# Two-layer diffusion backbone on one core: six modulation blocks in the odd layer, softmax divisor in the turn, bias loads on ScalarE's queue

## The reference, cut to what matters

```python
def ada_modulation(cond, w_mod, b_mod):            # w_mod: 1024 x 6144, per layer
    m = jax.nn.silu(cond) @ w_mod + b_mod
    return jnp.split(m, N_MOD, axis=-1)            # sh1, sc1, g1, sh2, sc2, g2

def even_layer(...):
    h = modulate(rms_norm(x, norm_mix), sh1, sc1) @ w_in        # also for the context
    o_lat = concat([fourier_mix(u), neighbourhood_attention(q, k, v, kc, vc, rpb)])
    x = x + g1 * (o_lat @ w_out)
    x = x + g2 * swiglu(modulate(rms_norm(x, norm_ffn), sh2, sc2), w1, w3, w2)

def odd_layer(...):
    h = modulate(rms_norm(x, norm_mix), sh1, sc1) @ w_in        # q, k, v and u
    x = x + g1 * (concat([attention(q, k_all, v_all), s5_mixer(u, uc)]) @ w_out)
    x = x + g2 * moe_swiglu(modulate(rms_norm(x, norm_ffn), sh2, sc2), ...)

def one_block(q_blk):                              # both layers' softmax, in substance
    s = einsum(q_blk, k_all) * dh ** -0.5          # even layer: plus a bias cut from rpb, and a mask
    p = softmax(s)
    return einsum(p, v_all)
```

## Time and profile before

| | us |
|---|---|
| median of 3 runs | 1913.64 (1910.66 to 1914.75) |
| the profiled execution | 1914.57 |
| its span | 1912.7 |
| PE busy in it | 1814.9 (95%) |
| DVE, ACT, POOL busy | 1265.6, 1003.7, 312.3 |
| start to the end of the even layer's input projection | 0 to 163.98 |
| turn of q and k, Fourier part | 163.98 to 184.47 |
| even layer's attention | 184.47 to 262.25 |
| its output projection and dense part | 262.25 to 696.27 |
| odd layer's norm, input projection, turn | 696.27 to 789.20 |
| odd layer's attention and S5 | 789.20 to 847.70 |
| output projection, router, set-up of the experts | 847.70 to 911.13 |
| experts | 911.13 to 1912.70 |

### The profile page before, as it was taken

One profiled execution on the slowest core, in us unless ns is written; L12 is line 12 of the kernel. 1 busy time (PEld: TensorE's weight loads), 2 busy tenths in 40 slices (PEclk: granted clock), 3 DMA queues, 4 the chain that ended last, 5 costly groups with the idle time before them and its releaser, 6 DMA issues.

```text
span 1912.7 us, 25247 instructions
## 1 busy us (share of the span) xinstructions
PE 1814.9 (95%) x8938; PEld 1413.6 (74%) x8938; DVE 1265.6 (66%) x1329; ACT 1003.7 (52%) x1096; POOL 312.3 (16%) x584
## 2 busy tenths in 40 slices
PE   4999788999999989797999999999999999999998
PEld 2666444888888876465888888888888888888886
DVE  3243734442433234744998989989889898898997
ACT  3222423421312121363677767777777777776774
POOL 6887931011111124101000000000000000000000
PEclk8999899999999999897999999999999999999999
DMA  9788532122323151502799999999989999898994
GB/s 371 307 337 272 195 127 88 43 111 77 121 77 121 45 203 56 165 2 88 289 370 355 352 370 337 368 352 355 371 344 359 349 358 368 346 362 345 364 367 182
DMA packets 72374, 481.55 MB, mean 252 GB/s; under 512 B 8368, under 2 KB 11568, under 8 KB 17456
## 3 DMA queue, kind: packets, MB, share of 16 engines
q1 hardware_dynamic: 68720, 470.82, 64.5%
q0 software_dynamic: 2448, 7.61, 1.5%
q10 hardware_dynamic: 1136, 2.21, 0.4%
HBM read 473.29 MB, written 7.32 MB: 251 GB/s over the span
## 4 chain that ended last, share of the span: by engine, by line
PE 90%; DMA 3%; DVE 3%; POOL 2%; issue 1%; ACT 1%; SPq 0%; DVEq 0%; ACTq 0%; POOLq 0%
PE bank L1042 32%; PE bank L1056 16%; PE bank L775 12%; PE bank L745 4%; PE bank L804 3%; PE bank L792 3%; PE bank L625 3%; PE bank L840 2%; DMA ring<-in_ev_mod 2%; PE bank L563 2%; PE bank L1015 2%; PE bank L1025 1%; PE bank L713 1%; PE bank L605 1%; PE bank L696 1%
## 5 line engine op out<-in xcount | busy, mean ns | idle before, releaser
L1806 DVE TENSOR_TENSOR rest<-ring,WR 128x2048 fp32r<-128x2048 f32 x336 | 758.3, 2288 | 80.6 <-ACT WR L1373 80.1
L1373 ACT ACTIVATE WR<-ring 128x2048 fp32r<-128x2048 f32 x336 | 632.3, 1917 | 48.4 <-DMA ring<-in_experts 47.9
L1042 PE MATMUL bank<-WR,xer 128*128 128x512 f32 x1792 | 582.0, 397 | 0.8 <-DVE s5v L1967 0.8
L1042 PEld LDWEIGHTS bank<-WR,xer 128*128 128x128 f32 x1792 | 337.0, 188 | 70.3 <-issue 0.8
L1042 PE MATMUL bank<-rest,xer 128*128 128x512 f32 x896 | 349.5, 390 | 0.0
L1056 PE MATMUL bank<-WR,heTr 128*128 128x512 f32 x896 | 282.2, 392 | 0.0
L775 PE MATMUL bank<-hTr,WR 128*128 128x512 f32 x672 | 207.2, 390 | 0.0
L1056 PEld LDWEIGHTS bank<-WR,heTr 128*128 128x128 f32 x896 | 168.2, 188 | 34.6
L1042 PEld LDWEIGHTS bank<-rest,xer 128*128 128x128 f32 x896 | 169.1, 189 | 32.9
L1056 PE MATMUL bank<-rest,heTr 128*128 128x512 f32 x448 | 174.4, 389 | 0.0
L1658 DVE TENSOR_TENSOR rest<-ring,WR 128x2048 fp32r<-128x2048 f32 (+2 forms) x38 | 80.3, 2115 | 123.9 <-ACT WR L1298 123.6
(11 more groups left out here) (338 smaller groups left out, 2175.4 us busy)
## 6 DMA issues: line engine op xcount, KB each, us to landing
ring<-in_experts SPq DMA_DIRECT2D x336, 1024.0 KB, 4.8
ring<-in_ev_mod SPq DMA_DIRECT2D x24, 1024.0 KB, 9.0
ring<-in_od_mod SPq DMA_DIRECT2D x24, 1024.0 KB, 8.6
ring<-in_ffn_up SPq DMA_DIRECT2D x22, 1024.0 KB, 6.8
ring<-in_ffn_down SPq DMA_DIRECT2D x12, 768.0 KB, 5.1
ring<-in_ev_in SPq DMA_DIRECT2D x8, 1024.0 KB, 6.7
ring<-in_ev_out SPq DMA_DIRECT2D x4, 1024.0 KB, 8.5
ring<-in_od_out SPq DMA_DIRECT2D x4, 1024.0 KB, 13.5
```

Of the source, the lines that this page charges most:

```text
L1042: mm = pe.matmul(bank[m % 2][:, :], xer[:, i, 4 * kh + k, :], w[j][:, 512 * k:512 * k + 512], start=(kh == 0 and k == 0 and x == 0), stop= ...
L1373: act.activation(part(0, h), ring[:, h % HALVES, :], ACT.Copy).then_inc(split_hi, 1)
L1806: dve.tensor_tensor(part(1, h), ring[:, h % HALVES, :], part(0, h).bitcast(F32), ALU.subtract).then_inc(split_lo, 1)
```

## The change

1. **Modulation.** Blocks 12 to 17 stay in the even layer, as group (12, 18); blocks 18 to 23 become a fourth group, (18, 24), in the odd layer: two in `turn_odd` (before its first and its fourth step) and four in the attention, behind the scores of rounds 0, 1, 2 and 4. Their loads stand on SP's queue in the odd layer. The even layer now has 12 blocks in its input projection, 1 in the turn, none in the Fourier part, 1 in the attention. ACT loads the condition vectors a second time (`late_cond`, a new input) and applies Silu in the dense part.
2. **Softmax divisor.** DVE no longer scales the probabilities. It scales the 128 x 128 identity by 1/sum into one of three buffers (`inverse`), and PE turns the probabilities by a matmul with it in place of a transpose. DVE waits for `prob_turned` before it overwrites a buffer, as ACT's exp does.
3. **Bias rows.** The DMAs move from POOL's queue to ACT's, with three raw buffers in place of two: heads 0 to 2 behind input jobs 8, 9 and 12, heads 3 and 4 in the Fourier part, heads 5 to 7 at the head of rounds 1 to 3. POOL's order after table 11 is: heads 2 and 3, table 12, heads 4 and 5, table 13, heads 6 and 7, tables 14 and 15.
4. **Waits that these need.** PE waits for the late condition vectors and for two banks before `turn_odd`, and for the fourth group's end (`mod_ready`, 2) before the first S5 output, since they share banks 6 and 7.

```diff
+EARLY = ([("mod", s) for s in range(4)]
+         + [("in", 0), ("mod", 4), ("mod", 5), ("in", 1), ("mod", 6), ("mod", 7), ("mod", 8), ("in", 2),
+            ("mod", 9), ("mod", 10), ("mod", 11), ("in", 3)]
+         + [("mod", s) for s in range(12, 18)])
+UNDER_TURN = {1: 16}
+UNDER_FOUR = {}
+UNDER_ATTN = {1: 17}
+MOD_GROUPS = ((0, 4), (4, 12), (12, 18), (18, 24))
+ODD_TURN = {0: 18, 3: 19}
+ODD_ATTN = {0: 20, 1: 21, 2: 22, 4: 23}
...
             sp.dma_start(U, scr_u.rearrange("(a b) c -> a b c", b=CHUNK)).then_inc(u_landed, 16)
+            for n in range(2):
+                load(S_LATE + n, a["od_mod"][6 + n])
             sp.wait_ge(lag_ready, 1)
...
                              src).then_inc(t_landed, 16)
+            for n in range(2, 6):
+                load(S_LATE + n, a["od_mod"][6 + n])
             for n in range(2):
                 load(S_OUT_O + n, a["od_out"][n])
...
+                        elif r in ODD_ATTN:
+                            modulation(ODD_ATTN[r])
...
-                                mm = pe.transpose(bank[3 + i % 2][:, c * P:(c + 1) * P],
-                                                  prob[:, i % 3, c * P:(c + 1) * P], ident)
+                                mm = pe.matmul(bank[3 + i % 2][:, c * P:(c + 1) * P],
+                                               prob[:, i % 3, c * P:(c + 1) * P], inverse(steps, i),
+                                               start=True, stop=True)
...
+                        if steps is ODD_STEPS and r == ODD_ROW + 1:
+                            modulation_turn(3)
...
+                    if jj in ODD_TURN:
+                        modulation(ODD_TURN[jj])
...
                     pe.wait_ge(t_landed, 16 * CHUNK)
+                    pe.wait_ge(mod_ready, 2)
...
+            def load_bias(h):
+                if h >= 3:
+                    act.wait_ge(bias_ready, h - 2)
+                for t in range(2):
+                    for q in range(2):
...
+                        act.dma_start(bias_raw[h % 3][64 * q:64 * q + 64, t * SEQ:(t + 1) * SEQ]
+                                      .rearrange("p (r c) -> p r c", r=ROWS), src).then_inc(bias_landed[h % 3], 16)
...
+                    if v in (5, 6):
+                        load_bias(v - 2)
...
+                    if steps is EVEN_STEPS and 1 <= r < 4:
+                        load_bias(4 + r)
...
-                            dve.tensor_scalar(prob[:, i % 3, 0:keys], prob[:, i % 3, 0:keys], rinv[:, i % 4:i % 4 + 1],
+                            if i >= 3:
+                                dve.wait_ge(prob_turned, i - 2)
+                            dve.tensor_scalar(inverse(steps, i), ident, rinv[:, i % 4:i % 4 + 1],
                                               None, ALU.mult).then_inc(prob_ready, 1)
```

More of the change, by code:

```diff
@@ L66 @@
 ROW_JOB = 9
-S_MOD = [EARLY.index(("mod", s)) for s in range(24)]
+S_MOD = [EARLY.index(("mod", s)) for s in range(18)]
 S_IN_E = [EARLY.index(("in", n)) for n in range(4)]
-MOD_GROUPS = ((0, 4), (4, 12), (12, 24))
-S_OUT_E, S_FFN = 28, 30
+MOD_GROUPS = ((0, 4), (4, 12), (12, 18), (18, 24))
+LATE = 18
+ODD_TURN = {0: 18, 3: 19}
+ODD_ATTN = {0: 20, 1: 21, 2: 22, 4: 23}
+ODD_ROW = max(ODD_ATTN) + 1
+S_OUT_E, S_FFN = 22, 24
 S_IN_O = S_FFN + UP_SLOTS + DOWN_SLOTS
-S_OUT_O = S_IN_O + 4
+S_LATE = S_IN_O + 4
+S_OUT_O = S_LATE + 6
+S_MOD += [S_LATE + n for n in range(6)]
 S_MOE = S_OUT_O + 2
@@ L212, in build @@
         silc = cond.rearrange("p (k s) -> p k s", s=62)
+        late_more = sb("late_more", [P, 84])
+        late_cond = [B[:, 11008:11260], late_more[:, :]]
+        silc_late = [x.rearrange("p (k s) -> p k s", s=42) for x in late_cond]
         hT = HT[:, :].rearrange("p (c t) -> p c t", c=DC)
@@ L228, in build @@
         bias = [S[:, at:at + 512] for at in (0, 512, 4608, 5120)]
-        bias_raw = B[:, 8192:9216].rearrange("p (b n) -> p b n", b=2)
+        bias_raw = [B[:, at:at + 512] for at in (8192, 8704, 10368)]
         prob = S[:, 1024:2560].rearrange("p (b n) -> p b n", b=3)
@@ L562, in modulation @@
                         c = 4 * i + j
-                        mm = pe.matmul(o[32 * j:32 * j + 32, :], silc[:, c, at:at + 32], w[:, c, :],
+                        x = (silc[:, c, at:at + 32] if s < LATE else
+                             silc_late[c // 6][:, c % 6, at - 20:at + 12])
+                        mm = pe.matmul(o[32 * j:32 * j + 32, :], x, w[:, c, :],
                                        start=(s == lo and i == 0), stop=(s == hi - 1 and i == 1))
@@ L981, in _ @@
             w_in_odd()
+            pe.wait_ge(late_ready, 1)
+            pe.wait_ge(in_normed, 15)
+            pe.wait_ge(in_copied, 15)
             turn_odd()
@@ L1303, in _ @@
             squares(1)
+            act.dma_start(late_cond[0], a["late"][:, 0:252]).then_inc(late_landed, 16)
+            act.dma_start(late_cond[1], a["late"][:, 252:336]).then_inc(late_landed, 16)
             modulate(1)
@@ L1324, in _ @@
                     gate_row(1, u)
+                if u == 5:
+                    act.wait_ge(late_landed, 32)
+                    act.activation(late_cond[0], late_cond[0], ACT.Silu)
+                    act.activation(late_cond[1], late_cond[1], ACT.Silu).then_inc(late_ready, 1)
             act.activation(warm[:, 0:1], cst[:, C_ONE:C_ONE + 1], ACT.Sqrt)
@@ L1641, in attention @@
                             modulation_row(2)
+                        if steps is ODD_STEPS and r == ODD_ROW:
+                            modulation_row(3)
                     if r >= 2:
@@ L2103, in _ @@
             pool.wait_ge(s5_raw, 32)
[L2104 to L2121 removed]
+            def head_bias(h):
+                pool.wait_ge(bias_landed[h % 3], 64 * (h // 3 + 1))
                 if h == 2:
@@ L2161, in _ @@
                 table(k)
-            head_bias(2)
-            head_bias(3)
-            for k in range(12, 16):
+            for h in range(2, NA_HEADS):
+                head_bias(h)
+                if h in (3, 5):
+                    table(12 + h // 4)
+            for k in range(14, 16):
                 table(k)
-                head_bias(k - 8)
             for i in range(2):
@@ L2284, in host_layout @@
     arrays = {"cond": cond.reshape(P, 62 * DC), "vec": v, "cst": constants(), "dft": dft_constants(), "rpb": rpb,
-              "s5b": bb.reshape(P, 2 * UNITS * S5_DIM), "s5c": cc.reshape(P, 2 * UNITS * S5_DIM)}
+              "late": np.ascontiguousarray(cond[:, :, 20:62]).reshape(P, 42 * DC), "s5b": bb.reshape(P, 2 * UNITS * S5_DIM), "s5c": cc.reshape(P, 2 * UNITS * S5_DIM)}
     def slots(w, cols):
```

52 lines of the change are left out of this document (22 added, 30 removed).

## The result

The changed kernel takes 1931.81 us in the median of 4 runs (1929.19 to 1935.67), the kernel before 1912.15 in the same comparison: ratio 1.0105, interval 1.0091 to 1.0119. The direction was forecast, the size was not: 1931.8 lies 7 us above the forecast of 1924.8 and just outside its range.

The account below looks back on a forecast made before the run. PE was taken to bound the input projection, and PE's waits to matter in the attentions. From 1914.6, -14.0 (even half) and +25.1 (odd half) gave 1925.7, less 0.9 to the median: 1924.8 us, range 1912 to 1931.

Parts of the forecast that it names:

- The odd layer: Odd layer: PE waits for late loads of blocks 20 to 22, plus dearer turns; +25.1 us (+19 to +28).
- rival A: Odd attention: the blocks' landing isn't the bound; odd half +15.6, time 1915.3 us, change not slower; chance 0.15.
- The turn by a matmul: Both attentions: a turn of eight by float32 matmuls takes 1.9 us rather than 1.0, +0.9 each.
- C: Turns in both attentions: a matmul costs no more than a transpose; -2.5 and -6.6, time 1915.7 us; chance 0.05.
- Input projection, Fourier part: Even layer before its attention: input projection -5.0 us, turn of q and k +0.3, Fourier part +0.8.
- The even attention: Even layer's attention: blocks leaving, waits going, dearer turns, ACT issues and stalls sum to -10.1 us (-16 to -5).
- the first of part 3: Even attention: with the DMAs off POOL, PE's three long waits should go, -10.4 us.
- The even half: Even layer as a whole, input projection to attention: -14.0 us (-21 to -8).
- +2 for this: Even attention: stalls that stay between DVE and POOL, +2 us (0 to +6).
- +2 for it: Even attention, rounds 1 to 3: ACT's bias issues for three heads, +2 us (0 to about +4.5).
- the four blocks: Even attention: four of five modulation blocks go, each worth 1.2 to 1.9 us, taken as -6.2.
- D: Even layer: ACT's issues delay exp and DVE still stalls on POOL; even half -8, time 1930.8 us; chance 0.08.

Follow-up runs that it names:

- the run with the blocks read later: Changed kernel with block 20 read behind round 3's scores, 21 behind round 4's, 22 and 23 behind round 5's, loads unchanged: 1928.92 us, ratio 1.0078.
- part 3 alone: Kernel before with only the bias rows' change (issued by ACT, POOL's tables 12 to 15 between the heads): 1921.90 us, ratio 1.0051.
- The run with gaps: Kernel before with a wait for itself behind each of four POOL table operations that had none: 1914.20 us, ratio 1.0016.
- the run with the tables elsewhere: Kernel before with ACT issuing the bias rows and POOL's last four tables computed ahead of head 2's bias row: 1910.44 us, ratio 1.0000.
- parts 2 and 3: Kernel before with the scaled identity in the turn and the bias rows issued by ACT, without the late blocks: 1928.09 us, ratio 1.0091.

## Where the forecast held, and where it was wrong

**The odd layer: right.** Forecast +25.1, measured +26.0. Measured from the end of the dense part, round 3 of the attention came 17.4 later than before (forecast 16.6), and from there to the output projection 8.6 was added (forecast 8.5). The landings were taken from what stood at the same place of the queue: block 22 came 117.1 after the dense part, against a forecast of 116.2. Three details were off. The wait stood almost wholly at block 20; block 21 had none, because block 20's matmuls at the half clock and the scores behind them took until it had landed. Blocks 18 and 19 weren't hidden where they stand: PE still waits (3.35) ahead of block 18, and the stages up to the attention grew by 4.0. All of that lies in front of the same landing, so the sum held. And the wait was worth less than the prediction had it. Its rival A, the odd layer without the wait, was 9.5 cheaper (25.1 less 15.6); the run with the blocks read later has no wait for a load and is 4.5 cheaper in the attention, with some 3 more lost to the half clock. Most of the 26.0 is the blocks and the turns, and they would have stayed.

**The turn by a matmul: right.** Two times a transpose, as the row of plain matmuls said; alone it cost 8.65 for a forecast of 8.7. (Its share in the odd layer stands in the prediction with three values, 5.7 in the sum, where the wait hides rounds 0 to 2, 6.2 in rival A and 6.6 in C; alone it was 7.1.) The four-fold ratio that the Trainium skill, page "TensorE: Matmul & The Clock Gate", section "Terms", gives for float32 did not show: 2.05 for a turn of eight against 1.09 for the transposes.

**Input projection, Fourier part: right** to 1 us each (the Fourier part with the turn of q and k).

**The even attention: wrong, by 12 us.** The term that failed is the first of part 3, "the long waits 3.66 + 2.42 + 4.33 = 10.4 should go", taken in full with no worse end; the runs showed part 3 alone lengthening this stage by 4.0. The even half as a whole came to -3.7, outside its own -21 to -8. That range was also tighter than the ends of its own terms: with the blocks at -4.7, ACT at +4.5 and the stalls at +6 the attention comes to -2.1, not -5. Three readings were behind it.

First, the scaling of 4.08 us was put down mostly to the DMA issues that POOL was making. POOL's timeline of the kernel before has only the first 0.6 us of it beside issues, and the rest beside arithmetic:

```profile
205.48 2.44 POOL L2112 DMA_DIRECT2D B<-in_rpb  x4
207.93 1.28 POOL L2128 TENSOR_TENSOR S<-B,cst 128x512 f32<-128x512 f32 x1
...
211.07 0.85 POOL L2149 TENSOR_TENSOR rows<-rows 128x288 f32<-128x288 f32 x1
```

The run with gaps kept those issues and halved the scaling; the run with the tables elsewhere brought it to 1.5. It is POOL's arithmetic back to back, which part 3 did not move out of the attention: in the changed kernel POOL waited idle for 18.5 us ahead of it, and did its tables inside. I had +2 for this with an upper end of 6.

Second, ACT's issues. The price of one was read where few were outstanding and multiplied. With heads in successive rounds the second half of a head took 7.93 (10.6 and 10.9 in the kernels with parts 3 and 2 + 3). I had +2 for it, with 4.5 as the end; in the changed kernel ACT's queue is behind 4.11 + 1.2 of PE's waits. Spacing the same issues took the long ones away. The range did not hold the time because this end was taken by multiplying a price, with no allowance for issues that get longer.

Third, the four blocks hid more than the idle of a steady round (0.74), by which they were priced. Head 7's row was late from POOL's whole program, and they hid part of that; and the block of round 0 filled the gap before the first exp, so that its going gave nothing (1.92 of work went, and the wait grew from 0.29 to 2.15). Alone the move gained 1.2, not 6.2. In the changed kernel part 3 does free head 7's row, so there the blocks gave 5.7. That is one reason why the parts don't add.

The Trainium skill, page "SBUF — State Buffer", section "Who interferes with whom", has both halves: a `tensor_scalar` inside SBUF can hold the ports that DVE shares with GpSimd, and the other engine then blocks fully; and a DMA of GpSimd's that a DVE operation holds up can be moved to a hardware queue. The rows agree with the first (3.99 us for a 128x128 scaling; 0.28 alone); the second speaks of DMAs that are held up, and it was DVE's operation that was late here. I weighed them evenly, and "no row tells them apart" was wrong: the POOL rows beside the two long scalings were there to be read. The Trainium skill, page "DMA: Bandwidth & Descriptors", section "Issuing engines are not separate DMA queues", says that the time to initiate a DMA is usually small relative to the DMA itself; the rows show 0.65 and, late in a close series, 4.0 to 5.4 each.

**Rivals.** A (the landing isn't the bound) fell, with a wait of 7.62. D, which priced ACT's issues and DVE's stalls at +6 together and ended at 1930.8, had the right mechanism, with a chance of 0.08. That its time is only 1.0 us from the result is in part luck: its even half is -8 where -3.7 was measured, and the 4.3 missing came back in the two stages that nothing was forecast for.

## What to carry to other kernels

Price a moved DMA issue by the queue that it joins, not by one issue: ask how many stand close together there, and what stands in order behind the issuing engine. Before filler work is taken out of a stage, find the longest wait that it hides, and who is late there. And when an engine idles just ahead of a stage in which it is in the way (POOL, 18.5 us), try moving its work forward: with that, a wait for itself behind each of POOL's table operations, and the bias rows issued where they hold nobody back, this kernel came out 0.5% faster, with nothing moved on PE.

## What the runs showed of the hardware

A DMA issue on ACT's queue took 0.65 us for a piece-wise 64 KB transfer, but in four kernels the last two issues of the fourth or fifth head within some 25 us took 7.93, 10.30, 10.64 and 10.89 us together. The DMA view of the stretch 160 to 222 us, for the changed kernel (its packets, then the queues of SP and of ACT), shows how finely those twenty issues are cut: 5440 packets for 1.31 MB, some 240 bytes each.

```profile
DMA packets 6845, 10.08 MB, mean 163 GB/s; under 512 B 5638, under 2 KB 5638, under 8 KB 5957
...
q1 hardware_dynamic: 1001, 7.23, 30.0%
q10 hardware_dynamic: 5440, 1.31, 11.9%
```

That is 272 packets a transfer. In the kernel before, the same stretch has twenty bias issues on POOL's queue, and that queue has 1200 packets in all (`q0 software_dynamic: 1200, 3.38, 22.2%`). Seven table transfers take some 560 of them, at the 80 each that five take in the changed kernel (399), so a bias transfer has about 32 (an estimate). The same pattern issued by ACT is cut into eight to nine times as many packets, which may be why its issues get long; that was not tried apart from the spacing.

DVE's scaling of 128x128 took 0.28 alone and 3.99 (changed kernel) or 5.43 (parts 2 and 3) beside POOL operations that stand back to back, and there it ended where POOL's stream had its first gap. The two long ones of 128x512 in the kernel before ended 0.5 us ahead of that gap. With waits of POOL for itself between operations these two went from 4.17 and 4.08 to at most 2.29.

A wait of 1.0 us in the odd attention (late blocks read later) was followed by a stretch with a mean granted clock of 0.69, which held some matmuls at 1.2 GHz; the next 11 us were at 2.4 GHz. Waits of 1.20 (changed kernel, at 807.91) and 1.26 (kernel before, at 843.20) were followed by matmuls of the full-clock length, so what lowers the clock stays open.
